# GpSimd's order of weight sums: the next set's third sum ahead of the first sum of the set behind it

## The reference, cut to what matters

```python
def swiglu(x, w_gate, w_up, w_down):
    return (jax.nn.silu(x @ w_gate) * (x @ w_up)) @ w_down
...
        x = x + 0.5 * swiglu(rms_norm(x, g_norm[l, 0]), w_ffn_gate[l, 0], w_ffn_up[l, 0], w_ffn_down[l, 0])
        h = rms_norm(x, g_norm[l, 1])
        ... (attention of the layer, added to x)
        x = x + 0.5 * swiglu(rms_norm(x, g_norm[l, 2]), w_ffn_gate[l, 1], w_ffn_up[l, 1], w_ffn_down[l, 1])
```

## Time and profile before

| | |
|---|---|
| runs, median (lowest to highest) | 2457.02 us (2455.48 to 2464.59) |
| the profiled execution | 2457.78 us |
| its span on the core | 2455.7 us |
| TensorE, busy share of the span | 98% |
| VectorE, ScalarE, GpSimd | 76%, 54%, 22% |
| DMA, mean | 136 GB/s |

### The profile page before, as it was taken

The page is one execution under the profiler, slowest core; times in us unless marked ns, Lnnn a source line. Parts: engine busy times, 40 slices in busy tenths (PEclk is TensorE's granted clock), DMA queues, the critical chain, the costliest instruction groups (busy, mean ns, idle before and its releaser), DMA issues. The chain is left out here.

```text
span 2455.7 us, 48881 instructions
## 1 busy us (share of the span) xinstructions
PE 2402.1 (98%) x18377; PEld 2261.9 (92%) x18377; DVE 1858.7 (76%) x3709; ACT 1336.1 (54%) x2873; POOL 544.4 (22%) x422
## 2 busy tenths in 40 slices
PE   9899999999999999999999999999999999999998
PEld 9899999888778999999988999999996699999998
DVE  7887979422787888787925889787928878887865
ACT  6555656201785655555622655555618856555554
POOL 1222222354000121222135222222131002222210
PEclk9999999999999999999999999999999999999999
DMA  5557575333863465756523775766467544766642
GB/s 146 121 116 144 106 148 101 95 116 97 304 237 94 97 140 103 144 115 140 104 79 127 187 143 115 139 127 126 107 227 265 209 112 94 145 125 126 139 101 82
DMA packets 423237, 334.20 MB, mean 136 GB/s; under 512 B 20641, under 2 KB 383834, under 8 KB 423010
## 3 DMA queue, kind: packets, MB, share of 16 engines
q1 hardware_dynamic: 281296, 246.98, 32.2%
q0 software_dynamic: 133136, 65.82, 21.9%
q10 hardware_dynamic: 8578, 18.37, 2.1%
HBM read 314.98 MB, written 16.13 MB: 135 GB/s over the span
## 5 line engine op out<-in xcount | busy, mean ns | idle before, releaser
L997 PE MATMUL PS<-x_area,w_area 128*128 128x320 f32 x3096 | 483.1, 310 | 2.3 <-ACT PS L1804 2.3
L997 PEld LDWEIGHTS PS<-x_area,w_area 128*128 128x128 f32 x3096 | 461.6, 188 | 2.7 <-ACT PS L1804 2.6
L1718 ACT ACTIVATE w_area<-R 128x512 fp32r<-128x512 f32 (+2 forms) x583 | 325.5, 567 | 204.9 <-DVE R L2414 92.3
L2393 DVE TENSOR_TENSOR w_area<-R,w_area 128x512 fp32r<-128x512 f32 (+2 forms) x583 | 357.7, 615 | 87.1 <-ACT w_area L1718 86.5
L2393 DVE TENSOR_TENSOR r_area<-R,r_area 128x512 fp32r<-128x512 f32 (+2 forms) x437 | 265.8, 617 | 94.4 <-ACT r_area L1718 88.8
L1804 ACT ACTIVATE PS<-PS 128x320 f32<-128x320 f32 x438 | 178.3, 416 | 215.6 <-PE PS L997 189.9
L997 PE MATMUL PS<-r_area,w_area 128*128 128x320 f32 x1584 | 266.4, 311 | 10.7 <-ACT PS L1804 6.2
L1718 ACT ACTIVATE r_area<-R 128x512 fp32r<-128x512 f32 (+2 forms) x437 | 247.7, 567 | 47.2 <-DVE R L2414 20.2
L997 PEld LDWEIGHTS PS<-r_area,w_area 128*128 128x128 f32 x1584 | 239.1, 188 | 18.3 <-ACT PS L1804 11.2
L1226 PE MATMUL PS<-w_area,xn_hi 128*128 128x512 f32 x800 | 251.5, 396 | 0.5 <-DVE xT L2578 0.3
L997 PE MATMUL PS<-r_area 128*128 128x320 f32 x1392 | 236.5, 311 | 2.2 <-DVE r_area L2648 1.8
(11 more groups left out here) (348 smaller groups left out, 4152.6 us busy)
## 6 DMA issues: line engine op xcount, KB each, us to landing
R<-in_w_ffn_up_dram SPq DMA_DIRECT2D x45, 512.0 KB, 5.2
R<-in_w_ffn_gate_dram SPq DMA_DIRECT2D x43, 512.0 KB, 5.1
R<-in_w_ffn_up_dram SPq DMA_DIRECT2D x86, 256.0 KB, 4.1
R<-in_w_ffn_up_dram POOLq DMA_DIRECT2D x86, 256.0 KB, 4.8
R<-in_w_ffn_gate_dram SPq DMA_DIRECT2D x82, 256.0 KB, 4.6
R<-in_w_ffn_gate_dram POOLq DMA_DIRECT2D x81, 256.0 KB, 5.5
R<-in_w_ffn_down_dram SPq DMA_DIRECT2D x52, 384.0 KB, 3.9
R<-in_w_ffn_down_dram SPq DMA_DIRECT2D x88, 192.0 KB, 3.7
```

Of the source, the lines that this page charges most:

```text
L997: last = pe.matmul(PS[:, bank, 0:HT], a[:, k, :], b, start=(start and opens), stop=(k == n - 1 and a is lo), skip_group_check=True)
L1718: act.activation(role_parts(f, g, s, role)[0], role_source(f, g, s, role), ACT.Copy).then_inc(sem("early_cast") if key in EARLY_COUNT else ...
L2393: dve.tensor_tensor(lo, role_source(f, g, s, role), hi.bitcast(F32), ALU.subtract).then_inc(sem("early_split") if key in EARLY_COUNT else ...
```

## The change

In add_sums, within a block. Before, the order was: first sums of sets 0 and 1, and then for each set n its third sum and the first sum of set n + 2. After, for n = 0 the third sum of set 0, the third sum of set 1 and the first sum of set 2; for each further n the third sum of set n + 1, and then the first sum of set n + 2. The waits of each sum are as before.

```diff
--- before.py
+++ after.py
@@ -875,8 +875,12 @@
                 order = chain(f)
                 for at in order[:2]:
                     first_sum(at)
+                ahead = [at for at in order[1:] if True]
                 for n, at in enumerate(order):
-                    third_sum(at)
+                    if at not in ahead:
+                        third_sum(at)
+                    if n + 1 < len(order) and order[n + 1] in ahead:
+                        third_sum(order[n + 1])
                     if n + 2 < len(order):
                         first_sum(order[n + 2])
 
```

## The result

The changed kernel takes 2523.73 us (median of 4 runs, 2520.29 to 2524.46) against 2457.51 us before (4 runs): ratio 1.0261, 95% interval 1.0239 to 1.0284. It is slower, as forecast, but by 66 us instead of 23, and outside the stated range of 2457 to 2502. Its profiled execution took 2520.29 us, its span is 2518.2 us.

The account below looks back on a forecast made before the run. TensorE, busy in 98% of the span, was taken to bound the kernel; its waits count. Terms 16.5 + 6.4 + 2 - 1.7 = 23.2 us on 2457.8 gave 2481.0, stated as 2480 us, range 2457 to 2502.

Parts of the forecast that it names:

- Term 1: Second set of the 11 three-pair down products: late first sum delays TensorE 1.5 us each, 16.5 us (bounds 3 and 30).
- The landing L: Second set of three-pair down products: needed first sum, issued at 1091.33, lands at 1097.0; TensorE resumes 1.18 us later.
- Term 2: The four two-pair down products: third sums stand closer than the loop between second sums, 1.6 us lost each, 6.4 us.
- Term 3: Third set of the 11 three-pair down products: late first sum costs 0.2 us each, 2 us (bounds 0 and 11).
- Term 4: Ends of two-pair products and start of a block: third sums go ahead of first sums, gain 1.7 us (bounds 0, -5).

Follow-up runs that it names:

- e2: The changed order for down sets alone (opening ones too), gate and up sets in the old order: 2517.56 us, 1.0233 of the kernel before.
- e3: The changed order for one set of each down product alone, the one behind the opening set (15 of 146 sets): 2501.84 us, 1.0169 of the kernel before.
- e4: Changed kernel, but in non-opening down sets low half of S3 goes ahead of next second sum, second row copy ahead of next S1 cast: 2483.4 us, 1.0102 of before.
- e11: Kernel before with low half of S3 and second row copy moved ahead in non-opening down sets, changed GpSimd order in gate and up sets alone: 2460.28 us, 0.9998.

## Why the prediction was wrong

*What bounds the kernel, and where the change bites.* Right. TensorE's waits decide; gate and up sets cost next to nothing (1.0012, but for one wait of 3.4 us at the start of the third block and the four first gate sets behind two-pair products); the loss is behind the opening down sets, and e2, e3 and e4 show the chain: late first sum, second sum and S1 cast, low half of S3 and row copy, TensorE.

*Term 1 (16.5 us), mis-sized.* Measured 28.4 us in these sets. TensorE's waits there grew by 24.4 us, 2.2 us a place, where 1.5 were forecast. The landing L was 7.2 us after the second sum in the forecast and 7.7 us in the trace (the first sum left 0.8 us behind the third, not 1.27, but took 6.6 us to land, not 5.7), and 9.0 to 9.3 us at two of the places. The prediction had the better figure in hand, the 6.3 us of the earlier trace rows, and went below it. The remaining 4.0 us are half-speed matmuls: these sets spend 10.8 us at the lower clock. The 1.18 us from the second sum's start to TensorE's restart held to 0.01 us.

*Term 2 (6.4 us), mis-sized.* Measured 17.9 us in the second to fourth sets of the two-pair products, and 3.4 us in the first gate sets behind them. TensorE's waits grew by 10.5 us in those down sets; the rest is mostly the clock, 17.9 us of them at the lower level.

*Term 3 (2 us).* Right as to waits, of which there are none, and wrong as to time, 9.5 us: the clock.

*Term 4 (-1.7 us).* Not seen as a gain. Single waits went (0.4 us at the second set of the third block), but the set behind it waits 3.4 us, where the first sum of the next set took 11.9 us to land.

*The step that failed most is a sentence under the sum:* "TensorE is busy everywhere else, so nothing makes the stalls good later." It takes a stall at its own length. Behind most stalls of 2 to 4 us TensorE ran at the lower clock for a while, as in the set behind the wait at 1121.68. That was 22 of the 62 us, and no term or rival had it. Without it the forecast's way of counting, with the measured waits, ends at 2457.8 + 40 = 2498 us, inside the range. The trace before held a hint that wasn't read: its 23.0 us at the lower clock, one stretch of it right behind the longest of its waits in a set, 2.3 us up to 72.95. It was no more than a hint: the same wait stands in the trace after, at 72.79, without such a stretch.

*The landing.* The prediction weighed what the Trainium skill says ("DMA: Bandwidth & Descriptors", section "Two DMAs through the same engine are not ordered"), that descriptors of one queue start in order and are pipelined, and took it to mean a landing as of a lone transfer. The section gives no time for a landing, and the reading didn't hold: 6.6 us instead of 3.8. Shortening the transfer ahead took 0.6 us off, shortening the load beside it 0.7 us; so what is in flight with it counts, and the larger part of the 2.8 us stays open.

## What to carry to other kernels

Before an instruction is put behind another one's wait on an in-order engine, follow it to its last user, through every engine on which something is queued behind what waits for it: here a transfer issued later held up, two engines on, a product half that didn't need it. A stall of TensorE can cost more than its length: behind 16 of the 20 longest in the sets here (1.8 to 4.0 us) the clock was at the lower level for a while. Count both, and look at the granted clock in the windows behind each long wait. And in a fixed order, put what the bounding engine needs ahead of what waits for a transfer: two such moves made the kernel before 0.3% faster. Look for the pattern everywhere: where e4 and e11 left one row copy behind a cast that waits, TensorE waited.

## What the runs showed of the hardware that was not expected

Useless matmuls in a wait paid: 304 more matmul records and 13.4 us less. Behind the wait of 1.88 us at 1121.68 the granted clock was 0.57 in the next 4 us; behind the one of 0.25 us at the same place before it was 1.00. With the wait filled, 0.73 us of it left, the clock stayed at 1.00. It is not a matter of the length alone: the wait of 2.79 us at 201.85 had 1.00 in the 4 us behind it (202 to 206). And a small accumulating transfer (192 KB) that landed in 3.8 us by itself (DMA share 0.42 from 1081 to 1085) took 6.6 us directly behind another of its queue and beside SyncE's loads (0.77 from 1114 to 1121).
